# Two transformer blocks on one core: the SBUF addresses of activations and split weights are moved

## The reference

```python
def reference(x, ...):
    x = first_block(x, ...)    # h + hybrid_mixer(rms_norm(h)); h + sq_relu_mlp(rms_norm(h)); rms_norm
    return second_block(x, ...)

def hybrid_mixer(u, w_in, ...):        # w_in 1024 x 3584
    z = u @ w_in                       # short convolution on one half,
    ...                                # chunked retention with 4 heads on the other
    return jnp.concatenate([y_conv, y_ret], axis=-1) @ w_out

def sq_relu_mlp(u, w_up, w_down):      # 1024 -> 4096 -> 1024
    hdn = jax.nn.relu(u @ w_up)
    return (hdn * hdn) @ w_down

def second_block(x, c, ...):
    ada = (c @ w_ada + b_ada)[:, None, :]          # six vectors: shift, scale, gate, twice
    ...
    h = rmsnorm(x, g_norm1) * (1.0 + scale1) + shift1
    proj = h @ w_in                    # 8 heads of attention with forget gates, 8 of top-128
    ...                                # attention with an indexer, two output gates
    x = x + gate1 * (merged @ w_out)
    h2 = rmsnorm(x, g_norm2) * (1.0 + scale2) + shift2
    x = x + gate2 * (jnp.square(jax.nn.relu(h2 @ w_mlp1)) @ w_mlp2)
    return rmsnorm(x, g_final)
```

## Time and profile before

| | us |
|---|---|
| median of 3 runs | 1353.09 |
| the three runs | 1352.45, 1353.96, 1353.09 |
| span of the profiled execution, first to last instruction | 1351.4 |
| PE busy (matmuls; records overlap) | 1340.5 |
| PEld busy (LDWEIGHTS) | 1093.9 |
| DVE / ACT / POOL busy | 754.1 / 526.0 / 563.0 |

### The profile page before, as it was taken

The page is one execution under the profiler, slowest core; times in us unless marked ns, Lnnn a source line. Parts: engine busy times, 40 slices in busy tenths (PEclk is TensorE's granted clock), DMA queues, the critical chain, the costliest instruction groups (busy, mean ns, idle before and its releaser), DMA issues.

```text
span 1351.4 us, 18070 instructions
## 1 busy us (share of the span) xinstructions
PE 1340.5 (99%) x6380; PEld 1093.9 (81%) x6380; DVE 754.1 (56%) x1085; ACT 526.0 (39%) x830; POOL 563.0 (42%) x230
## 2 busy tenths in 40 slices
PE   9999999999999999999999999999999999999998
PEld 8888878888888888876877777888878888888886
DVE  3555578475664654878788774444463241432355
ACT  6344234322323324254366655322355133142333
POOL 5334334453553635524222223444434534345351
PEclk9999999999999999999999999999999999999999
DMA  7232245555665655423222323333423423324231
GB/s 230 79 93 83 90 124 167 167 172 174 197 175 163 176 150 163 112 92 96 62 63 79 95 64 94 109 94 109 125 71 102 125 76 111 93 79 123 78 94 63
DMA packets 212807, 155.74 MB, mean 115 GB/s; under 512 B 8932, under 2 KB 193760, under 8 KB 212744
## 3 DMA queue, kind: packets, MB, share of 16 engines
q1 hardware_dynamic: 212280, 154.43, 39.5%
q10 hardware_dynamic: 464, 0.48, 0.1%
HBM read 152.75 MB, written 4.74 MB: 117 GB/s over the span
## 4 chain that ended last, share of the span: by engine, by line
PE 53%; DVE 1%; ACT 1%; issue 0%; POOL 0%; ACTq 0%; DVEq 0%
PE ps L580 28%; PE ps L1126 11%; PE ps L1070 3%; PE ps L1007 2%; PE ps L986 1%; PE ps L973 1%; PE ps L1156 1%; PE ps L959 1%; PE ps L960 1%; PE ps L963 0%; PE ps L946 0%; PE ps L920 0%; PE ps L921 0%; PE ps L924 0%; DVE nt L2267 0%
## 5 line engine op out<-in xcount | busy, mean ns | idle before, releaser
L541 POOL TENSOR_TENSOR w_lo<-raw,w_hi 128x1024 fp32r<-128x1024 f32 x222 | 560.0, 2530 | 758.2 <-ACT w_hi L1212 738.1
L580 PE MATMUL ps<-u_hi,w_hi 128*128 128x512 f32 x944 | 378.3, 401 | 0.7 <-POOL w_lo L541 0.5
L580 PE MATMUL ps<-u_hi,w_lo 128*128 128x512 f32 x944 | 368.4, 390 | 0.0
L580 PE MATMUL ps<-u_lo,w_hi 128*128 128x512 f32 x944 | 367.8, 390 | 0.0
L1212 ACT ACTIVATE w_hi<-raw 128x1024 fp32r<-128x1024 f32 x222 | 231.6, 1053 | 290.7 <-PE ps L580 112.5
L580 PEld LDWEIGHTS ps<-u_hi,w_lo 128*128 128x128 f32 x944 | 177.2, 188 | 37.7
L580 PEld LDWEIGHTS ps<-u_hi,w_hi 128*128 128x128 f32 x944 | 178.2, 189 | 36.1 <-issue 1.6
L580 PEld LDWEIGHTS ps<-u_lo,w_hi 128*128 128x128 f32 x944 | 177.6, 188 | 35.2 <-issue 1.0
L580 PE MATMUL ps<-y_hi,w_hi 128*128 128x512 f32 x320 | 125.2, 391 | 0.1
L580 PE MATMUL ps<-y_hi,w_lo 128*128 128x512 f32 x320 | 124.5, 389 | 0.0
L580 PE MATMUL ps<-y_lo,w_hi 128*128 128x512 f32 x320 | 124.5, 389 | 0.0
(11 more groups left out here) (317 smaller groups left out, 1878.4 us busy)
## 6 DMA issues: line engine op xcount, KB each, us to landing
raw<-w_in SPq DMA_DIRECT2D x69, 512.0 KB, 3.8
raw<-w_mlp SPq DMA_DIRECT2D x64, 512.0 KB, 4.0
adaw<-w_ada SPq DMA_DIRECT2D x32, 768.0 KB, 4.5
raw<-w_up SPq DMA_DIRECT2D x32, 512.0 KB, 6.6
raw<-w_down SPq DMA_DIRECT2D x32, 512.0 KB, 6.0
raw<-w_out SPq DMA_DIRECT2D x16, 512.0 KB, 4.4
bias_rows<-bias_rows SPq DMA_DIRECT2D x4, 635.0 KB
xtok<-x SPq DMA_DIRECT2D x4, 512.0 KB, 7.5
```

The lines of the kernel that those rows point to most:

```text
L541: pool.tensor_tensor(w_lo[:, s, :], raw[:, s, :], w_hi[:, s, :], ALU.subtract).then_inc(lo_ready[s], 1)
L580: last = pe.matmul(ps[0:cols, bank, :], w[:, s, c], r[:, k, :], start=(k == ks[0] and w is w_hi and r is r_hi), stop=(k == ks[-1] and w is ...
```

## The change

The small tiles are allocated first, followed by 72 unused values (288 bytes), which brings `xres` to 20480 = 10 x 2048. All large tiles keep their order. Between `raw` and `w_hi` 16 unused values (64 bytes) are put in. No instruction is added, removed or moved: in the built program the instructions and the waits of every engine are, row by row, those of before; addresses alone differ.

```diff
+ALIGN = 72
...
-        xres = sb("xres", [P, KC, T])
-        u_hi, u_lo = sb("u_hi", [P, KC, T], F32R), sb("u_lo", [P, KC, T], F32R)
-        y_hi = sb("y_hi", [P, KC, T], F32R)
...
-        y_lo = sb("y_lo", [P, KC, T], F32R)
-        raw = sb("raw", [P, SLOTS, KC * P])
-        w_hi, w_lo = sb("w_hi", [P, SLOTS, KC * P], F32R), sb("w_lo", [P, SLOTS, KC * P], F32R)
         small = sb("small", [P, SMALL])
...
         top8 = sb("top8", [P, 8])
+        sb("align", [P, ALIGN])
+        xres = sb("xres", [P, KC, T])
+        u_hi, u_lo = sb("u_hi", [P, KC, T], F32R), sb("u_lo", [P, KC, T], F32R)
+        y_hi = sb("y_hi", [P, KC, T], F32R)
...
+        y_lo = sb("y_lo", [P, KC, T], F32R)
+        raw = sb("raw", [P, SLOTS, KC * P])
+        sb("shift", [P, 16])
+        w_hi, w_lo = sb("w_hi", [P, SLOTS, KC * P], F32R), sb("w_lo", [P, SLOTS, KC * P], F32R)
         odd = ExitStack()
```

More of the change, by code:

```diff
@@ L240, in build @@
         top8 = sb("top8", [P, 8])
+        sb("align", [P, ALIGN])
+        xres = sb("xres", [P, KC, T])
+        u_hi, u_lo = sb("u_hi", [P, KC, T], F32R), sb("u_lo", [P, KC, T], F32R)
+        y_hi = sb("y_hi", [P, KC, T], F32R)
+        scores = ExitStack()
+        sb("y_lo_front", [P, NQ, T], where=scores)
+        work = sb("work", [P, NT - 1, T], where=scores)
+        rfin = sb("rfin", [P, T], where=scores)
+        scores.close()
+        y_lo = sb("y_lo", [P, KC, T], F32R)
+        raw = sb("raw", [P, SLOTS, KC * P])
+        sb("shift", [P, 16])
+        w_hi, w_lo = sb("w_hi", [P, SLOTS, KC * P], F32R), sb("w_lo", [P, SLOTS, KC * P], F32R)
         odd = ExitStack()
```

## The result

The changed kernel takes 1377.85 us, the median of 4 runs (1377.39 to 1379.87), against 1353.53 us of the kernel before (4 runs): a ratio of 1.0183 (95% interval 1.0171 to 1.0195). It is slower by 24 us. The span of its profiled execution is 1375.6 us, 24.2 more than before; that execution took 1377.43 us, so 1.8 us lie around the span, as in the kernel before.

What follows compares the result with a forecast made beforehand. PE's step from one matmul start to the next was taken as the bound. From a span of 1351.4 us, 33.5 and 1.3 were subtracted, giving 1316.6; with 1.7 us above the span, 1318 us. The range reached from below 1295 to 1368.

Steps and rivals of the forecast that it cites:

- the forecast: Step of `u` and `y` matmuls with split weights falls to 217 to 224 ns; 1318 us in all, chance 0.38.
- Part (b): `m` comes to the residue of the weights, 64 mod 2048; its 192 matmuls step at 226.7 ns, 1.3 us gained.
- Part (c): Activation rows no longer run across a multiple of 2048; claimed to be worth zero.
- Part (d): DVE, ACT and POOL access 0 mod 64 instead of 32; any change is covered by PE, so no effect.
- (a): Activations and split weights no longer start alike: 5028 matmuls gain 6.67 ns each, 33.5 us; bounds 56.8 gained, 33.7 lost.
- the collision: In float32r matmuls, moving and stationary reads get in each other's way, causing at least part of the 13.3 ns addition.
- all of it: Rival: the two read streams come free of each other, step about 215.3 ns, 1295 us; chance 0.18.
- the settled step is lost: Rival: in `unit` and `down_rows` steps rise to 232 to 233.4 ns, 1379 to 1386 us; chance 0.20.
- The test that I proposed against myself: If `unit` and `down_rows` part company, the moving tile's absolute address counts, not how the two tiles stand to each other.

Runs made afterwards that it cites:

- the two halves of the change: Changed kernel without the 64 unused bytes: 1352.07 us; kernel before with only those 64 bytes ahead of `w_hi`: 1378.65 us.
- the exchange of roles: Changed kernel with activations at 64 and split weights at 256 mod 2048, reversing their starts modulo 256: 1366.75 us, ratio 1.0099.
- the rows of matmuls alone: Separate kernel without the transformer: 72 float32r matmuls per line at chosen moving and stationary starts, no other engine working; 226.7 ns a step at difference 0, multiples of 32.
- 32/32: Setting of the matmul-only kernel, moving and stationary tile both starting 32 bytes behind their multiples of 2048 and 512: 226.7 ns a step.
- 0/64: Setting of the matmul-only kernel, moving tile starting at 0 bytes, stationary at 64: 233.3 ns a step with 512 by 128 columns.
- 0/0: Setting of the matmul-only kernel, moving and stationary tile both starting at 0 bytes: 226.7 ns a step with 512 by 128 columns.

## Why the prediction was wrong

The time of 1378 us lies above the range, which ended at 1368, and on the other side of the forecast.

**Right, and shown.** That PE's step is the only thing that the change can touch: PE's waits are unchanged and the steps account for the loss (25.1 us less the 1.3 of `m`), but for 1.6 us that the fall of the clock added in the profiled execution. That the step depends on addresses, that `m` against `u` is the evidence, and that it is a matter of how the moving tile stands to the stationary one: the two halves of the change, the exchange of roles and the rows of matmuls alone show it. Part (b), `m` down to 226.7 ns, -1.3 us: 43.54 us measured for the forecast 43.5. (What it says of `k_both` against `q_up` and `q_dn` is a slip without weight: these start alike before, at 1760, and after, at 64, and the sums of their steps moved by less than 0.2 us.) Part (c), nothing for the multiples of 2048: without the 64 bytes all long pieces had the step of before. Part (d), nothing from DVE, ACT and POOL: POOL even waits longer for ACT than in the earlier trace rows, 767.5 us in place of 738.1.

**Wrong: the choice inside the bounds of (a).** "The one difference that the rows show between two addresses is just such a block, and two are there to lose." The pair of bounds was -56.8 and +33.7 us, and no row had float32r tiles 64 bytes apart. I took a point on the side of the gain with an argument on blocks of 64 bytes read per row, as if equal starts were the collision and neighbouring blocks the way out. Measured, that term is +28.9 us by the settled steps in place of -33.5, and 25.1 by the sums of all starts without the fall of the clock. Nothing that was tried at 512 by 128 columns was below the step of equal starts. The argument fails twice. The 33rd block of `m` is not what made it slow: 32/32, with 33 blocks too, has 226.7 ns, and 0/64, with 32, has 233.3. And two of the observations that I had put down to the collision spoke against the gain: only equal starts had the low value in the trace, and the one pair with unequal starts was slower. By that row alone the nearest value for a new, unequal pair was +6.7 ns; I named it as the end of the range that "nothing excludes" and then gave it one chance in five.

The other comparison behind (a) and "all of it", plain float32, holds for a record (429.2 ns alone), not for a matmul: the two records of 512 columns in the earlier trace rows are one matmul, 858 ns, so its columns go at a quarter of the full rate and not at half of it. It said nothing of what float32r can reach, and no setting came near the 215.3 ns that were read from it.

**The rival that came true** is the third, "the settled step is lost", priced at 1379 to 1386 us. It was over by some us because it took one price for both shapes of product, while those with the weights moving lose 2.3 ns only; and because part of the matmuls of `unit` stood at 232 ns before. Its words, that the streams "may lock higher or not at all", fit in their second half: `unit` mostly alternates between 231 and 236 ns, `down_rows` runs through a cycle of 226, 229 and 232 ns. Two streams of reads as the reason are not shown.

**The test that I proposed against myself** was that `unit` and `down_rows` part company, and then "an absolute address counts". They did part, and still it was not the absolute address: the exchange of roles shows that the sign of the difference counts. The two readings could not be told apart by the changed kernel alone.

**The rule of the Trainium skill** that PE has two independent read ports and never waits on anyone (SBUF — State Buffer, "Who interferes with whom"), read as "the loading of the stationary operand costs nothing at any address", would have given 1352 us. The measurements decide against that reading for float32r, in that the address of the stationary operand alone changes the step (0/0 against 0/64); whether it is the ports that make it so is not shown. For bfloat16 and plain float32 no row here contradicts it.

A version that is no slower than either kernel is the change without its 64 bytes, 1352.07 us, or with 256, 1352.27: 1.3 and 0.9 us, 0.1%, below the kernel before, with intervals that end at 0.9997 and 0.9999.

## What to carry to other kernels

Where PE is the bound, divide a long piece of the chain of waits by its matmuls for each kind of product; two values for one shape, type and clock mean that the shape alone does not set the step, and here it was the addresses of the tiles. Look at the granted clock in short stretches: 40 slices hid a fall of 3.4 us. For float32r products of 512 by 128 columns let the moving and the stationary tile start at the same residue modulo 256, multiples of 32 bytes (at 448 or 256 columns that is not the best); a small tile that is put between them, of 64 or 128 bytes, cost 1.8% of this kernel. And a term whose ends have both signs should go to the row that is nearest in kind, not to a picture of the mechanism that no row has tested.

## What the runs showed that I had not expected

- The step of float32r matmuls (512 moving, 128 stationary columns) depends on the difference of the two starts with a period of 256 bytes and a sign: 226.7 ns at 0, 228.9 at +64, 233.3 at -64, without any other engine at work.
- Settled is often a cycle: 226, 229, 232 ns at +64, 231 and 236 (or 233 and 234) at -64, and at one offset the same code took either 43.96 or 44.80 us for 192.
- At the half clock (426 to 427 ns a step) float32r had no addition, although the starts were unequal.
- Fewer stationary columns make the step longer, not shorter (231.7 ns with 32, 226.7 with 128, at equal starts); bfloat16 has 216 ns a matmul, plain float32 429.2 a record and 858 a matmul, at each of the offsets tried.
